# One eighth of one expert's down weights, fetched row group by row group

## The reference

```python
def moe(h, router_w, router_b, w_gate, b_gate, w_up, b_up, w_down, b_down):
    hf = h.reshape(b * s, d)                              # 256 x 1024
    logits = (hf @ router_w + router_b).astype(jnp.float32)
    top_val, top_idx = lax.top_k(logits, TOP_K)           # 4 of 32
    probs = jax.nn.softmax(top_val, axis=-1)
    combine = jnp.sum(jax.nn.one_hot(top_idx, N_EXPERTS, dtype=jnp.float32) * probs[..., None], axis=1)
    y = jnp.zeros((b * s, d), jnp.float32)
    for e in range(N_EXPERTS):                            # 32
        gate = jnp.minimum(hf @ w_gate[e] + b_gate[e], SWIGLU_LIMIT)
        up = jnp.clip(hf @ w_up[e] + b_up[e], -SWIGLU_LIMIT, SWIGLU_LIMIT)
        act = gate * jax.nn.sigmoid(SWIGLU_ALPHA * gate) * (up + 1.0)
        y = y + combine[:, e:e + 1] * (act @ w_down[e] + b_down[e])
    return y.astype(h.dtype).reshape(b, s, d)
```

## Time and profile before

| | |
|---|---|
| median of 3 runs | 1163.77 us (1163.21 to 1164.88) |
| the profiled execution, its own time | 1162.5 us |
| its span in the trace | 1160.7 us |
| PE busy | 1116.7 us (96%) |
| DVE, ACT busy | 367.0 us (32%), 257.4 us (22%) |
| read from HBM | 443.47 MB |
| chain of work that ended last | PE 74%, DMA 23% |
| rate of the transfers in the experts' part | 421 to 433 GB/s in most of the 40 slices |
| granted clock of PE | 0.98 of full, mean |

### The profile page before, as it was taken

The page is one execution under the profiler, slowest core; times in us unless marked ns, Lnnn a source line. Parts: engine busy times, 40 slices in busy tenths (PEclk is TensorE's granted clock), DMA queues, the critical chain, the costliest instruction groups (busy, mean ns, idle before and its releaser), DMA issues.

```text
span 1160.7 us, 15023 instructions
## 1 busy us (share of the span) xinstructions
PE 1116.7 (96%) x6113; PEld 557.2 (48%) x6113; DVE 367.0 (32%) x896; ACT 257.4 (22%) x526; POOL 15.6 (1%) x20
## 2 busy tenths in 40 slices
PE   8999999999999999898989998999999998999998
PEld 8998989864343434242423343334333433443333
DVE  5477765642323222122221221121212221222213
ACT  6466555340210111011111111111110111110112
POOL 1000000000000000000000000000000000000000
PEclk9999999999999999999999999999999998999999
DMA  9856567799999999999999999999999999999995
GB/s 286 275 170 188 171 205 281 302 402 409 414 420 423 423 431 432 432 431 433 431 430 429 432 432 430 433 431 429 432 432 432 430 432 431 429 427 429 422 423 232
DMA packets 53933, 445.52 MB, mean 384 GB/s; under 512 B 3842, under 2 KB 32184, under 8 KB 36592
## 3 DMA queue, kind: packets, MB, share of 16 engines
q1 hardware_dynamic: 51818, 439.83, 91.4%
q0 software_dynamic: 1248, 4.20, 1.4%
q10 hardware_dynamic: 806, 0.59, 0.2%
HBM read 443.47 MB, written 1.13 MB: 383 GB/s over the span
## 4 chain that ended last, share of the span: by engine, by line
PE 74%; DMA 23%; DVE 1%; SPq 1%; issue 0%; ACT 0%; DVEq 0%
PE psum L1419 27%; DMA ring<-in_w_up 20%; PE psum L1454 14%; PE psum L1039 5%; PE psum L1338 5%; PE psum L1040 5%; PE psum L1041 5%; PE psum L1353 4%; DMA ring<-in_w_down 3%; PE psum L1361 2%; PE psum L1086 1%; PE psum L1179 1%; SPq L564 1%; PE psum L1155 1%; PE psum L1346 1%; PE psum L1133 1%
## 5 line engine op out<-in xcount | busy, mean ns | idle before, releaser
L1419 PE MATMUL psum<-ring,xT 128*64 128x512 f32 x960 | 434.7, 609 | 34.6 <-DMA ring<-in_w_up 34.6
L1420 PE MATMUL psum<-ring,xT 128*64 128x512 f32 x960 | 434.8, 609 | 0.0
L1419 PEld LDWEIGHTS psum<-ring,xT 128*64 128x64 f32 x960 | 132.2, 140 | 312.0 <-issue 287.9
L1454 PE MATMUL psum<-ring,guT 128*64 128x512 f32 x984 | 226.5, 602 | 0.4 <-DVE guT L1938 0.4
L1919 DVE COPY gu<-psum 128x512 f32<-128x512 f32 x32 | 33.5, 1047 | 570.3 <-PE psum L1420 570.3
L1420 PEld LDWEIGHTS psum<-ring,xT 128*64 128x64 f32 x960 | 132.2, 140 | 0.0
L1454 PEld LDWEIGHTS psum<-ring,guT 128*64 128x64 f32 x984 | 65.5, 137 | 135.7 <-issue 112.2
L978 ACT COPY gu<-psum 128x512 f32<-128x512 f32 x32 | 34.0, 1062 | 420.0 <-PE psum L1420 420.0
L1608 DVE TENSOR_TENSOR low<-raw,high 128x2048 fp32r<-128x2048 f32 x31 | 71.3, 2300 | 36.3 <-ACT high L771 36.3
L1039 PE MATMUL psum<-hT_hi,high 128*128 128x256 f32 x272 | 78.3, 288 | 0.1
L1040 PE MATMUL psum<-hT_lo,high 128*128 128x256 f32 x272 | 76.9, 283 | 0.0
(11 more groups left out here) (212 smaller groups left out, 1029.2 us busy)
## 6 DMA issues: line engine op xcount, KB each, us to landing
ring<-in_w_down SPq DMA_DIRECT2D x25, 4096.0 KB, 20.4
ring<-in_w_up SPq DMA_DIRECT2D x24, 4096.0 KB, 28.4
ring<-in_w_gate SPq DMA_DIRECT2D x23, 4096.0 KB, 29.8
ring<-in_w_gate SPq DMA_DIRECT2D x12, 2048.0 KB, 19.2
raw<-in_w_in SPq DMA_DIRECT2D x22, 1024.0 KB, 5.4
ring<-in_w_up SPq DMA_DIRECT2D x10, 2048.0 KB, 22.6
ring<-in_w_down SPq DMA_DIRECT2D x7, 2048.0 KB, 12.1
ring<-in_w_up SPq DMA_DIRECT2D x12, 1024.0 KB, 10.3
```

The costliest lines, as they stand in the source:

```text
L1419: mm(every(bank(GU + nb)[0:CAP, :]), x_k, of_chunks(gate[:, k, :], nb), start=k == 0, stop=k == KC - 1)
L1420: done = mm(every(bank(GU + nb)[CAP:P, :]), x_k, of_chunks(up[:, k, :], nb), start=k == 0, stop=k == KC - 1)
L1454: done = mm(o[half * CAP:(half + 1) * CAP, :], values[:, k, :], chunk_k[:, half * BANK:(half + 1) * BANK], start=k == 0, stop=k == KC - 1)
```

## The change

The load of m = 74 (expert 24's down matrix) is taken out of the loop. It becomes one load of the chunks 0 to 6 of all 128 partitions (28 KB each), and then 22 loads of chunk 7: 21 of six partitions each, and one of the last two. Each of those moves 4 KB per partition, and all of them count on a new semaphore, `rows_of`. PE waits for it beside `place_in[4]`, before the whole of expert 24's down product. The bytes are the same, and so is the arithmetic.

```diff
 AT_ONCE = 2
+BY_ROWS, ROWS = 3 * 24 + 2, 6
...
                 for m in range(3 * RING, TAIL):
-                    if not by_parts(m):
+                    if m == BY_ROWS:
+                        free(m, 1)
+                        load(m, 0, KC - 1, place_in[m % RING])
+                        e, kind = MATRICES[m]
+                        for r0 in range(0, P, ROWS):
+                            r = slice(r0, min(r0 + ROWS, P))
+                            sp.dma_start(ring[m % RING][r, KC - 1, :], weights_of[kind][e][r, KC - 1, :]).then_inc(rows_of, 16)
+                    elif not by_parts(m):
                         free(m, 1)
                         load(m, 0, KC, place_in[m % RING])
...
                 pe.wait_ge(place_in[i], 16 * (p * in_pass(i) + in_place(m)))
+                if m == BY_ROWS:
+                    pe.wait_ge(rows_of, -(-P // ROWS) * 16 * (p + 1))
```

More of the change, by code:

```diff
@@ L414, in build @@
         y_up, result_done, y_out = sem("y_up"), sem("result_done"), sem("y_out")
-        y_first, count_read = sem("y_first"), sem("count_read")
+        y_first, count_read, rows_of = sem("y_first"), sem("count_read"), sem("rows_of")
         block = ctx.enter_context(nc.Block())
```

## The result

| | before | changed |
|---|---|---|
| median, 10 runs each | 1163.57 us (1161.61 to 1164.88) | 1166.68 us (1164.96 to 1168.46) |
| ratio, 95% interval | | 1.0029 (1.0021 to 1.0038) |
| span of the profiled execution | 1160.7 us | 1164.4 us |
| granted clock, mean | 0.984 | 0.982 |

By the ratio the change costs 3.4 us (2.4 to 4.4); the two medians are 3.1 us apart. The forecast of 1169.7 us was 3 us too high. The range of 1165.8 to 1175.5 us held the time, near its lower end, and the sign was right.

The account below looks back on a forecast made before the run. The full DMA stream, making PE wait at expert 25, was taken as the bound. 1163.77 us plus 5.9 us for SP held gave 1169.7 us, the six engines' own time not adding; range 1165.8 to 1175.5 us.

Parts of the forecast that it names:

- the sign: Whole kernel: slower 0.83, same 0.14, faster 0.03.
- The bound and the place: Expert 25's start: PE waits 4.56 us for m = 76; stream delay shifts the end equally, idle growing to about 10.5 us.
- Which engines carry the loads: At the 22 loads: largest divisor up to 16 of the partitions, so six engines per six-partition load, two for the last.
- SP held at ten loads: At the 22 loads: SP is held when ten loads are under way, delaying m = 75; +5.9 us, chance 0.38.
- Three long issues: SP's tail: issues of 1.26, 7.43 and 2.12 us instead of 0.43, read as SP held with ten loads under way.
- The term of 5.9 us: Stream before m = 75: held row issues let it go on at 948.0 us instead of 942.1.
- The six engines' own time: At the 22 loads: six engines with 21 or 22 pieces of 4 KB fall back 2.1 to 5.5 us, 4.0 in the middle.
- Rival 2: At the 22 loads: SP is not held, the six engines are the bound; +4.0 us, 2.1 to 5.5, chance 0.27.
- rival 4: At the 22 loads: not slower, the six engines lead the slowest by 2.1 us or more; within 0.2 us, chance 0.12.
- the other ten get ahead: At the 22 loads: engines without row loads get ahead and gain nothing, since each load waits for its slowest engine.
- rival 3: At the 22 loads: six engines writing six neighbouring partitions get in each other's way; +8.5 us, up to +11.8, chance 0.20.

## Why the prediction was right or wrong

**The bound and the place: right.** Expert 25's wait on m = 76 took up the loss, and the end of the kernel moved by the same amount. The idle time grew by 3.6 us, the span by 3.7, the landing in the tail by 3.9. One reading was off without harm: from m = 73 to m = 74 it is 10.7 us, not 9.7, and the difference is the instruction packet at 935.3 us.

**Which engines carry the loads: right.** 128 further reports, six for each load of six. The trace's counts at the start of the kernel were enough.

**SP held at ten loads: wrong, and it was the likeliest case.** The step that failed is the transfer of a limit from the tail to here. Three long issues were explained by the number of loads under way, with the reservation that it might be pieces, and then this number was applied to loads of 24 KB. The runs with 22 and 64 loads show no hold by the number of loads, and an issue takes 0.30 to 0.34 us there instead of 0.48. The term of 5.9 us goes to zero. What holds SP in the tail was not tried. It is not the bytes under way: the ten loads there are 12 MB, and in the change the issue at 945.95 us takes 0.43 us with nearly 16 MB under way (its load lands 38 us later). The number of packets remains possible, of one engine or of all together.

**The six engines' own time: the mechanism right in part, the size accidental.** Rival 2 had 4.0 us from 22 x (0.15 + part of 0.15) - 1.2. Measured is 0.25 us for a piece and its report on the five leading engines, 22 x 0.25 - 1.2 = 4.3 us, and on the one that sets m = 76 4.2 - 1.2 = 3.0 us. But the extra over 0.15 us is not the report's: with a quarter of the reports the pace was the same, and an own piece takes 0.16 us with or without one. Rival 2's sign did not come either: the DMA share never fell to six sixteenths, because the ten others went on with m = 75.

**Three things that the sum had missed or put aside.** First the lead, rival 4: true, but as a part of the sum and not as a case for itself. Five of the six engines were 5 us or more ahead, and the length of their own work did not set m = 76; the sixth had a lead of 1.5 us. A full DMA share, held against rival 4, says nothing about leads: an engine that is ahead goes on with the next load. Second, and the greatest part, engines are slowed whatever they carry; the prediction put this at nothing ("the other ten get ahead"). It is 39 of the 50 us of engine time. The first load of m = 74, 28 KB on each partition, lands 22.2 us after its issue where with chunk 7 in one load it lands after 19.5. The ten engines have no row loads, and still the last of them is later. Third, what rival 3 was about is real in another form: not neighbours, but other engines' partitions, and not the six alone, but all 16. It had its price at 8.5 us because it took the six to be confined to a narrow way; 21 partitions apart they do just as badly, and 16 engines as badly as six.

**The chances.** Slower was given 0.83 and is what came. The value of 1169.7 us was the case that did not occur; rival 2's 1167.8 is 1.1 us above the measured median. The time lies in the range by rival 2's lower end, 1165.8 us, whose mechanism was right in part only. That it did is luck in good part.

## What to carry to other kernels

In a stream of loads that is full, the price of a small load lay here not in its issue or its report but in which engines carry it, and to which partitions; and it was paid mostly by the loads beside it. Keep loads at all 128 partitions, also small ones, and split along the free dimension. 512 KB in one load of 128 partitions cost nothing here; the same bytes in 2 to 64 loads of fewer partitions cost 3 to 6 us in ten of eleven forms and 1.9 in the eleventh. When a stream loses time, look at how long the untouched packets take, not only at the new ones. Reports counted in short windows tell which engines lead and by how much; such a lead hides a loss at the next landing, but here not at the end.

## What the runs showed of the hardware that was not expected

- The 16 engines drift apart in a full stream: the reports of one load come within 2.3 us at 341 us and over 6.4 us at 935 to 942 us. In this load, the three before it and the two behind it seven reports come first each time, within 0.7 us. A 16 KB packet of the instruction queue, one every 20 to 34 us, sets one engine back by about 1.6 us (1.1 us of its own and 0.5 us on the next piece); that the drift adds up from these is likely, not shown.
- A piece of 4 KB takes 0.16 us in a load of 128 partitions and 0.24 us on average in loads of six, and the rate of all 16 engines together is 319 GB/s from 934 to 944 us instead of 428. One engine with foreign pieces is enough to make the 32 KB pieces of all 15 others take 1.43 to 1.53 us instead of 1.22. That this goes by engine and partition is shown by the loads four apart (own pieces 0.16 us and all else undisturbed, foreign ones 0.3 us and all else at 2.2 us). That two loads of 64 lose as much as the change is not explained by a count of foreign pieces.
- SP's queue takes 64 loads of two partitions in 19.4 us, 0.30 us each, without a stop, with 42 of them under way. Loads of six partitions 21 apart take 0.70 us each to issue, neighbours 0.34.
- Left open: what holds SP's issues in the tail; what the engines share that one of them can slow all, and on which side of a transfer; why twice the change costs 9.8 us; whether foreign pieces of another size than 4 KB do the same; and why the one load of 102 partitions, with fewer reports and the same pieces, was the worst of those on six engines (1.0050).
